# Another bank pair for the second block's output openings, and other points for the last attention heads, in a two-block fp32 kernel

## The chip, the cores and the metric

One core of a Trainium2 chip runs the whole program. The metric is the device time of one execution in microseconds, as the median of three runs. Matmuls run in fp32r on operands split in two parts; weights stream from HBM.

## The reference

Two blocks over 512 tokens of width 2048. The first is one layer with dilated attention (16 heads of 64) and a gated recurrence (8 heads), the second has two layers, each with retention (6 heads), differential attention (4 heads) and a gated linear recurrence (LRU).

```
# first block
z = rmsnorm(h) @ w_in;  y_att = o_att * silu(ag);  y_hg = rmsnorm(o_fw + o_bw) * silu(hg)
h = h + rmsnorm([y_att, y_hg] @ w_out);  h = h + rmsnorm(sigmoid(h @ w_pg) * (p @ w_pp))
# second block, for l in 0, 1
proj = rmsnorm(x) @ w_in[l]
w    = softmax(q0 k0) - lam * softmax(q1 k1);  do = w @ v               # causal, 4 heads
diff = rmsnorm(do) * g * (1 - lam_init) * silu(dg)
lru  = rg_lru(lx) * silu(lg)
x    = x + rmsnorm([ret, diff, lru] @ w_out[l])
```

## The kernel before

Activations stand transposed, as 16 row tiles of 128 x 512 (`MIX`, `UH`, `UL`). A projection is a chain of output tiles. For one tile TensorE makes 16 x 3 matmuls of 128 x 128 by 128 x 512: weight high by operand high, high by low, low by high. They fall into four **quarters** of 12 matmuls (`quarter`, L276 on). SyncE loads a tile's weights into one of two `w_raw` buffers; ScalarE rounds them into `w_high` quarter by quarter (`high`, L644), GpSimd subtracts into `w_low` (L230), and SyncE loads the next but one when GpSimd has finished. Every handover is a counting semaphore; each engine's order is written out in the program. `w_free` counts quarters that TensorE has used up, `z_free` accumulator tiles that were read out.

A **step** is four tiles, so 16 quarters (points p = 0 to 15), and behind each quarter the helper functions put a piece of the previous head's attention. Which piece stands at which point is in the tables `GROUPED`, `LAST_PAIR` and `LAST_DIF` (L80 to L89). A head of differential attention has four query blocks a: scores into SC (L497), a bias and row minimum on VectorE (L1370), two exponentials on ScalarE (L795), the weighted difference on VectorE (L1381), a turn on TensorE (L516), a copy out on ScalarE, and values into the bank `OB` (L507). Then the squares of `OB` on ScalarE (L780), their sum by a matmul with ones (L345), its inverse root on ScalarE (L663, L665) and the output on VectorE (L1358, L1360). With `GROUPED`, half a head's last blocks, its squares, sum, root and output fall into the next step (`late`). The last head has no next step, so `LAST_DIF` brings it to an end within its own: sum and output at p = 15. Its step runs beside four LRU gate tiles, for which VectorE scales the tile (`rstd_mul`, L1173), bounds it (L1185), waits for ScalarE's three activations (L675 to L679) and multiplies twice (L1192, L1441). Two more gate tiles follow without a head.

The output projection **opens** with two tiles together (`two_tiles`, `pair_step`, L313 to L334): for each row k of the operand six matmuls into Z[0] and Z[1], with the first tile's weights in `out_weights`. So an opening needs both banks free, and the operand row by row: ScalarE's copy `u_high` (L656) and VectorE's low part `u_low` (L1460). Rows 6 to 9 are the differential heads, rows 10 to 15 the LRU. The accumulators alternate by tile: the last gate tile stands in Z[1]. In the first block the opening's pair steps themselves stand between the pieces of the last attention pair (`LAST_PAIR`); there ScalarE and VectorE prepare operand rows around the step before and this one, with `low_quarter(q)` for rows 4q to 4q + 3, and values of a pair go to `OB`, free when VectorE has written the previous pair's output (L1278).

The PSUM has eight banks: Z[0], Z[1], SC[0], SC[1], TP[0], TP[1], `OB`, and `VB`, which holds a head's turned V until ScalarE copies it at point 4.

Of the kernel before, what the change touches and what calls it, by code (L numbers as in the profile page):

```python
# [27 lines left out]
ALU = mybir.AluOpType  # L28
AX = mybir.AxisListType

P = 128
# [40 lines left out]
             if any(max(LRU_BW * n, P * a) < min(LRU_BW * (n + 1), P * (a + 1)) and  # L72
# [45 lines left out]
def build(nc, wt, xT, pT, pos1, pos2, par1, par2, dlam, gw, cst, idn, masks, bias, dec, cmask, out):  # L118
    ctx = ExitStack()
    with ctx:  # L120
# [76 lines left out]
        OUT_BANK = SC[0]  # L197
        LAST = [SC[0], SC[1], TP[0], OB, Z[0], Z[1]]
# [78 lines left out]
        def _(pe):  # L277
# [35 lines left out]
            def pair_step(t, k, gen):  # L313
# [17 lines left out]
            def two_tiles(t, gen):  # L331

                for k in range(KT):
                    pair_step(t, k, gen)  # L334
# [86 lines left out]
            def att_values(j, a):  # L421

                if a == 0:
                    pe.wait_ge(sem("vn_ready"), j + 1)
                    pe.wait_ge(sem("att_done"), PRIMED + j)
                for hd in range(2):
                    pe.wait_ge(sem(f"pte{hd}"), PRIMED + j * 4 + a + 1)
                for c in range(4):
                    for hd in range(2):
                        mm = pe.matmul(OB[64 * hd:64 * hd + 64, a * P:(a + 1) * P],  # L430
# [13 lines left out]
            def att_work(j, p, late=None, at=GROUPED):  # L444
# [13 lines left out]
                if p in at["values"] and at is not GROUPED:  # L458
                    att_values(j, at["values"][p])
# [63 lines left out]
            def dif_work(j, p, late=None, at=GROUPED):  # L523

                if p == 0:
# [5 lines left out]
                if p in at["values"] and at is GROUPED:  # L531
# [5 lines left out]
                if p in at["values"] and at is not GROUPED:  # L537
                    dif_values(j, at["values"][p])
                if late is not None and p == at["sums"]:
                    dif_sums(late)  # L540
                if p == 15 and at is not GROUPED:
                    dif_sums(j)
# [60 lines left out]
            for l in range(LAYERS):  # L603
# [16 lines left out]
                with pe.Fori(2, DIF_HEADS) as i:  # L620
# [3 lines left out]
                     late=l * DIF_HEADS + DIF_HEADS - 2, at=LAST_DIF)  # L624
# [13 lines left out]
        def _(act):  # L638
# [147 lines left out]
            def dif_work(j, p, late=None, at=GROUPED):  # L786

                if p in at["softmax"]:
# [20 lines left out]
                if p == 15 and at is not GROUPED:  # L809
                    dif_squares(j)  # L810
                    dif_root(j)
# [1050 lines left out]
```

## Time and profile before

| | us |
|---|---|
| median of three runs | 3239.13 (3238.85 to 3240.21) |
| the profiled execution | 3240.39 |
| its span, first to last instruction | 3238.6 |
| TensorE busy | 3087.8 (95%) |
| VectorE, GpSimd, ScalarE busy | 1685.2, 1308.0, 1186.2 |
| mean granted TensorE clock | 0.983 of full |

A time in the rows below is in microseconds from the span's start. The first block's opening stands near 1060 to 1105, those of the second block's layers near 2157 and 3037.

### The profile page before, as it was taken

The numbers are of one execution on the slowest core, as the hardware profiler recorded it, in microseconds if no ns is written. First come the engines' busy times: TensorE is split into PE (matmuls) and PEld (weight loads), VectorE is DVE, ScalarE is ACT, GpSimd is POOL, SyncE is SP. The second block draws the span as 40 slices with busy tenths as digits, with TensorE's granted clock in tenths as the row PEclk, the third lists the DMA queues.
The fourth block names the chain that finished last, engine by engine and source line by source line (L and its number), as shares of the span: only waits on it lengthen the run. The fifth ranks groups of instructions, "written<-read, shape, count | busy, mean of one in ns | idle before, by whom it ended". The sixth has DMA issues, their size and how long they took to land.

```text
span 3238.6 us, 44470 instructions
## 1 busy us (share of the span) xinstructions
PE 3087.8 (95%) x15326; PEld 2434.9 (75%) x15326; DVE 1685.2 (52%) x2260; ACT 1186.2 (37%) x2092; POOL 1308.0 (40%) x1004
## 2 busy tenths in 40 slices
PE   8999999999999999998999999989999999999897
PEld 6877777777777787877777777768777777777785
DVE  5576767645445514656565664451265556644412
ACT  5433333233333433343233333343332333343432
POOL 4433333333334244452434344344534434443444
PEclk9999999999999999998999999999999999999998
DMA  6222221121222223233322222223332222221322
GB/s 233 104 92 77 68 74 65 65 79 69 74 78 78 106 102 136 87 115 114 127 71 96 70 90 79 77 79 142 117 136 95 91 75 89 82 78 69 126 105 91
DMA packets 60374, 307.68 MB, mean 95 GB/s; under 512 B 5601, under 2 KB 5985, under 8 KB 28897
## 3 DMA queue, kind: packets, MB, share of 16 engines
q1 hardware_dynamic: 34848, 253.77, 22.1%
q10 hardware_dynamic: 25408, 52.37, 4.6%
q8 instruction: 71, 1.16, 0.1%
q14 instruction: 47, 0.38, 0.0%
HBM read 287.77 MB, written 18.35 MB: 95 GB/s over the span
## 4 chain that ended last, share of the span: by engine, by line
issue 58%; POOL 30%; PE 9%; POOLq 1%; DMA 1%; ACT 1%; DVE 1%; DVEq 0%; SPq 0%; ACTq 0%
POOL w_low L230 29%; PE z L293 8%; PE z L326 1%; DMA w_raw<-in_wt 1%; POOLq L229 1%; ACT u_high L656 0%; PE scores L293 0%; POOL next_weights L238 0%; DVE u_low L1460 0%; POOLq L264 0%; DVE work L1179 0%; POOLq L252 0%; ACT w_high L644 0%; DVEq L1751 0%; DVE work L1753 0%
## 5 line engine op out<-in xcount | busy, mean ns | idle before, releaser
L230 POOL TENSOR_TENSOR w_low<-w_raw,w_high 128x512 fp32r<-128x512 f32 x932 | 1247.9, 1343 | 1904.9 <-ACT w_high L644 1893.9
L293 PE MATMUL z<-u_high,w_high 128*128 128x512 f32 x3408 | 1382.2, 406 | 4.7 <-POOL w_low L230 4.0
L293 PE MATMUL z<-u_high,w_low 128*128 128x512 f32 x3408 | 1333.3, 391 | 0.0
L293 PE MATMUL z<-u_low,w_high 128*128 128x512 f32 x3408 | 1332.6, 391 | 0.0
L644 ACT ACTIVATE w_high<-w_raw 128x512 fp32r<-128x512 f32 x928 | 577.5, 628 | 1342.2 <-PE z L293 1209.8
L293 PEld LDWEIGHTS z<-u_high,w_high 128*128 128x128 f32 x3408 | 643.2, 189 | 152.7 <-issue 15.2
L293 PEld LDWEIGHTS z<-u_low,w_high 128*128 128x128 f32 x3408 | 643.5, 189 | 143.4 <-issue 14.4
L293 PEld LDWEIGHTS z<-u_high,w_low 128*128 128x128 f32 x3408 | 642.4, 189 | 137.4
L1477 DVE TENSOR_TENSOR work<-work 128x512 f32<-128x512 f32 x87 | 92.3, 1061 | 364.9 <-ACT work L875 351.6
L1173 DVE TENSOR_TENSOR work<-z,work 128x512 f32<-128x512 f32 x110 | 76.1, 692 | 185.8 <-PE z L293 143.4
L1201 DVE SCALAR_TENSOR_TENSOR work<-z,work 128x512 f32<-128x512 f32 x56 | 38.7, 692 | 186.7 <-PE z L293 185.9
L1179 DVE RECIPROCAL work<-work 128x512 f32<-128x512 f32 x40 | 134.1, 3353 | 3.3 <-issue 0.4
L1205 DVE SCALAR_TENSOR_TENSOR work<-z,work 32x512 f32<-32x512 f32 (+1 forms) x176 | 120.9, 687 | 2.4
L1242 DVE TENSOR_TENSOR work<-work 128x512 f32<-128x512 f32 x64 | 70.6, 1102 | 81.6 <-PE scores L388 74.8
L309 PE MATMUL z<-u_high,next_weights 128*128 128x512 f32 x192 | 71.7, 415 | 20.4 <-DVE u_low L1462 12.8
L656 ACT ACTIVATE work<-work 128x512 f32<-128x512 f32 x56 | 37.8, 674 | 116.2 <-DVE work L1246 116.2
L656 ACT ACTIVATE work<-turned 128x512 f32<-128x512 f32 (+2 forms) x100 | 53.5, 543 | 72.9 <-PE turned L441 43.3
L388 PEld LDWEIGHTS scores<-work 128*32 128x32 f32 (+2 forms) x1792 | 38.5, 120 | 49.6 <-DVE work L1256 23.1
L388 PE MATMUL scores<-work 128*32 128x32 f32 (+2 forms) x1792 | 46.3, 210 | 25.7 <-DVE work L1256 11.9
L1192 DVE TENSOR_TENSOR mixed<-work 128x512 f32<-128x512 f32 (+1 forms) x35 | 24.3, 694 | 85.5 <-ACT work L679 85.5
L1209 DVE TENSOR_TENSOR work<-work 128x512 f32<-128x512 f32 x56 | 64.5, 1152 | 5.2
L675 ACT ACTIVATE work<-work 128x512 f32<-128x512 f32 x48 | 30.2, 629 | 93.1 <-DVE work L1185 93.1
(241 smaller groups left out, 3088.2 us busy)
## 6 DMA issues: line engine op xcount, KB each, us to landing
w_raw<-in_wt SPq DMA_DIRECT2D x242, 1024.0 KB, 4.8
out_hT<-work ACTq DMA_DIRECT2D x10, 1024.0 KB, 6.9
work<-in_xT ACTq DMA_DIRECT2D x8, 1024.0 KB, 13.2
work<-out_hT ACTq DMA_DIRECT2D x8, 1024.0 KB, 10.3
e_scratch<-work ACTq DMA_DIRECT2D x1, 4096.0 KB, 17.0
work<-in_gw ACTq DMA_DIRECT2D x2, 1792.0 KB, 10.5
work<-in_dec ACTq DMA_DIRECT2D x12, 256.0 KB, 2.6
work<-rope_tables ACTq DMA_DIRECT2D x10, 256.0 KB, 2.9
```

What stands on the lines that cost most here:

```text
L230: pool.tensor_tensor(WL[:, 4 * q:4 * q + 4, :], RAW[:, t.odd, 512 * q:512 * q + 512].rearrange("p (k c) -> p k c", k=4), WH[:, 4 * q:4 * q ...
L293: mm = pe.matmul(bank[:], w[:, k, :], u[:, k, :], start=(k == 0 and n == 0), stop=(k == KT - 1 and n == 2))
L309: mm = pe.matmul(bank[:], w[x], u[:, k, :], start=(k == 0 and n == 0), stop=(k == KT - 1 and n == 2))
L388: mm = pe.matmul(bank[o:o + g, keys], kk, qq, start=True, stop=True)
L644: act.activation(WH[:, 4 * q:4 * q + 4, :], RAW[:, n.odd, 512 * q:512 * q + 512].rearrange("p (k c) -> p k c", k=4), ACT.Copy).then_inc(se ...
L656: i = act.activation(dst, src, ACT.Copy, **kw)
L1173: v.tensor_tensor(dst, (Z[t.odd] if bank is None else bank)[:], row(RSTD), ALU.mult).then_inc(sem("z_free"), 1)
L1179: v.reciprocal(row(r), row(r))
L1205: i = v.scalar_tensor_tensor(out=row(TM)[o:o + half], in0=z[x:x + half, :], scalar=-scale if first else scale, in1=row(sin)[o:o + half], o ...
L1209: v.tensor_tensor(row(dst), row(dst), row(TM), ALU.add)
L1242: v.tensor_tensor(x, x, y, ALU.mult)
L1477: i = v.tensor_tensor(row(ACC), row(ACC), row(SQ0 + s), ALU.add)
```

## The change

Nothing is added to the computation. Four things move:

1. The second block's openings write `Z[0]` and `VB` instead of `Z[0]` and `Z[1]`, and wait for one accumulator tile fewer. ScalarE reads the second tile from `VB`.
2. In the second block the last differential head uses `GROUPED`. Its values of block 2 and turn of block 3 stand behind quarter 0 of gate tile 4, its values of block 3 behind quarter 0 of tile 5, its sum behind quarter 1 of tile 5. On ScalarE its copy, squares and root stand between the pieces of the output operand, on VectorE its output between low parts 7 and 8.
3. The last attention pair of the first block puts its values into `VB`.
4. In the first block VectorE scales the last gate tile before it makes any low part; low quarters 0 to 3 stand at points 0 to 3 of the last pair's step.

```diff
-LAST_DIF = dict(scores={0: 0, 3: 1, 7: 2, 11: 3}, softmax={1: 0, 4: 1, 8: 2, 12: 3}, turn={3: 0, 6: 1, 10: 2, 14: 3},
-                values={5: 0, 7: 1, 11: 2, 15: 3}, turn_late={0: 3}, values_late={0: 2, 2: 3}, last=2, sums=3, out=4, v_copy=2)
...
+        FIRST = {1: [Z[0], Z[1]], 2: [Z[0], VB]}
...
-                    pe.wait_ge(sem("z_free"), t.times(1, -T_HGG))
+                    pe.wait_ge(sem("z_free"), t.times(1, -T_HGG if block == 1 else -T_HGG - 1))
...
-                        mm = pe.matmul(Z[x][:], w[x], u[:, k, :], start=(k == 0 and n == 0),
+                        mm = pe.matmul(FIRST[block][x][:], w[x], u[:, k, :], start=(k == 0 and n == 0),
...
-                    pe.wait_ge(sem("att_done"), PRIMED + j)
+                    if bank is OB:
+                        pe.wait_ge(sem("att_done"), PRIMED + j)
...
-                    att_values(j, at["values"][p])
+                    att_values(j, at["values"][p], VB)
...
                 for m in range(4, LRU_TILES):
                     for q in range(4):
                         quarter(Tile(T_L2 + R_LG + m, (PER_LAYER, l)), q)
+                        if (m, q) == (4, 0):
+                            dif_values(last, 2)
+                            dif_turn(last, 3)
+                        if (m, q) == (5, 0):
+                            dif_values(last, 3)
+                        if (m, q) == (5, 1):
+                            dif_sums(last)
...
                 for q in range(4):
                     high(t.plus(-2), q)
+                    if q == 0:
+                        dif_turned(last, 3)
...
+                    if q == 2:
+                        act.wait_ge(sem("dif_done"), PRIMED + last + 1)
                     for m in range(4 * q, min(4 * q + 4, 15)):
                         copy(UH[:, m, :], MIX[:, m, :], "uh_ready")
+                    if q == 0:
+                        dif_squares(last)
+                    if q == 1:
+                        dif_root(last)
...
-                 between={14: lambda: low_quarter(0), 15: lambda: low_quarter(1)})
...
-                 between={0: lambda: low_quarter(2), 2: lambda: low_quarter(3), 6: lambda: low_tile(14, 16, MIX[:], None)})
+                 between={0: lambda: low_quarter(0), 1: lambda: low_quarter(1), 2: lambda: low_quarter(2),
+                          3: lambda: low_quarter(3), 6: lambda: low_tile(14, 16, MIX[:], None)})
...
                 low(l * 32 + 64, MIX[:], b=8)
+                dif_out(l * DIF_HEADS + DIF_HEADS - 1, 9)
+                low(l * 32 + 64, MIX[:], a=8, b=12)
                 rstd_mul(Tile(T_L2 + R_LG + 5, (PER_LAYER, l)), row(RW))
                 bounded()
-                low(l * 32 + 64, MIX[:], a=8, b=12)
```

TensorE, last layer, around the last head's sum of squares (`turned<-work,ones`). Before, behind quarter 15 of the head's step, with the last values ahead of it:

```order
L293 MATMUL z<-u_low,w_high 128x512
L293 MATMUL z<-u_high,w_low 128x512
L507 MATMUL o_bank<-work 128x128 [waits dpte]
L507 MATMUL o_bank<-work 128x128 x3
L345 MATMUL turned<-work,ones 128x512 [waits dsq_ready]
L293 MATMUL z<-u_high,w_high 128x512 [waits l_ready,z_free]
L293 MATMUL z<-u_low,w_high 128x512
L293 MATMUL z<-u_high,w_low 128x512
```

In the changed program, behind quarter 1 of the last gate tile:

```order
L290 MATMUL z<-u_high,w_low 128x512
L290 MATMUL z<-u_high,w_high 128x512
L290 MATMUL z<-u_low,w_high 128x512
L290 MATMUL z<-u_high,w_low 128x512
L342 MATMUL turned<-work,ones 128x512 [waits dsq_ready]
L290 MATMUL z<-u_high,w_high 128x512 [waits l_ready]
L290 MATMUL z<-u_low,w_high 128x512
L290 MATMUL z<-u_high,w_low 128x512
```

The sum has moved six quarters on; its wait for the squares (`dsq_ready`) now stands inside the last gate tile.

ScalarE, last layer, from the fifth gate tile's activations to the first copies of operand rows 8 to 11. Before:

```order
L675 ACTIVATE work<-work 128x512 [waits g_bounded]
L677 ACTIVATE work<-work,ones 128x512
L679 ACTIVATE work<-work 128x512
L644 ACTIVATE w_high<-w_raw 128x512 [waits w_free,w_raw1]
L656 ACTIVATE u_high<-mixed 128x512 x4
L644 ACTIVATE w_high<-w_raw 128x512 [waits w_free,w_raw1]
L656 ACTIVATE u_high<-mixed 128x512 x4
L644 ACTIVATE w_high<-w_raw 128x512 [waits w_free,w_raw1]
L656 ACTIVATE u_high<-mixed 128x512 [waits lru_done]
```

In the changed program (`work<-o_bank` are the squares, `work<-turned,constants` and the row behind it the root):

```order
L678 ACTIVATE work<-work 128x512 [waits g_bounded]
L680 ACTIVATE work<-work,ones 128x512
L682 ACTIVATE work<-work 128x512
L647 ACTIVATE w_high<-w_raw 128x512 [waits w_free,w_raw1]
L659 ACTIVATE u_high<-mixed 128x512 x4
L783 ACTIVATE work<-o_bank 128x512 [waits dav_done,dif_done]
L647 ACTIVATE w_high<-w_raw 128x512 [waits w_free,w_raw1]
L659 ACTIVATE u_high<-mixed 128x512 x4
L666 ACTIVATE work<-turned,constants 128x512 [waits dss_done]
L668 ACTIVATE work<-work 128x512
L647 ACTIVATE w_high<-w_raw 128x512 [waits w_free,w_raw1]
L659 ACTIVATE u_high<-mixed 128x512 [waits dif_done,lru_done]
```

The squares stand behind the first high part of the second output tile and its four operand copies, the root behind the next four; the copies of rows 8 to 11 also wait for the head's output.

VectorE, first block, from the last step before the last pair into it. Before:

```order
L1214 COPY work<-work 128x512
L1215 COPY work<-work 128x512
L1460 TENSOR_TENSOR u_low<-mixed,u_high 128x512 [waits uh_ready] x8
L1173 TENSOR_TENSOR work<-z,work 128x512 [waits w_free]
L1185 TENSOR_SCALAR work<-work 128x512
L1288 ISA work,small<-scores,work 128x512 [waits s_done,ones_set]
L1288 ISA small 128x1
L1288 ISA work,small<-scores,work 128x512 [waits s_done,ones_set]
L1288 ISA small 128x1
L1273 COPY work<-turned 128x512 [waits av_done,pt_done]
L1460 TENSOR_TENSOR u_low<-mixed,u_high 128x512 [waits uh_ready] x4
```

In the changed program:

```order
L1225 COPY work<-work 128x512
L1226 COPY work<-work 128x512
L1184 TENSOR_TENSOR work<-z,work 128x512 [waits w_free]
L1196 TENSOR_SCALAR work<-work 128x512
L1299 ISA work,small<-scores,work 128x512 [waits s_done,ones_set]
L1299 ISA small 128x1
L1299 ISA work,small<-scores,work 128x512 [waits s_done,ones_set]
L1299 ISA small 128x1
L1284 COPY work<-turned 128x512 [waits av_done,pt_done]
L1470 TENSOR_TENSOR u_low<-mixed,u_high 128x512 [waits uh_ready] x4
L1304 RECIPROCAL small<-small 128x2 [waits exp_done]
L1307 TENSOR_SCALAR work<-work,small 128x512 x2
```

The scaling of the last gate tile (L1173, now L1184) stands first, and the eight low parts behind the turned copy (L1273, now L1284) and the first probabilities.

## Rows read from the trace of the kernel before

**Rows 1.** The page: section 1, and of section 6 the weight loads (KB each, us to landing).

```profile
PE 3087.8 (95%) x15326; PEld 2434.9 (75%) x15326; DVE 1685.2 (52%) x2260; ACT 1186.2 (37%) x2092; POOL 1308.0 (40%) x1004
...
w_raw<-in_wt SPq DMA_DIRECT2D x242, 1024.0 KB, 4.8
```

**Rows 2.** Waits of TensorE over the span: us in total, times, longest.

```profile
PE z L326 <- DVE work L1173: 18.1, 3, 7.4
...
PE o_bank L507 <- issue: 11.7, 2, 5.9
...
PE turned L516 <- DVE work L1381: 5.7, 4, 1.8
...
PE turned L345 <- ACT work L780: 1.5, 2, 0.7
```

**Rows 3.** TensorE's time line from 2961: start, duration, instruction, [idle before <- releaser].

```profile
2967.49 0.77 PE L507 MATMUL o_bank<-work 128*128 128x128 f32 x2 [5.85 <-issue]
2967.91 0.77 PE L293 MATMUL z<-u_high,w_high 128*128 128x512 f32 x1
...
2973.15 0.39 PE L516 MATMUL turned<-identity,work 128*128 128x128 f32 x2
```

**Rows 4.** TensorE's time line, later places of the same step and the opening.

```profile
2950.64 1.05 PE L507 MATMUL o_bank<-work 128*128 128x128 f32 x8
2951.45 0.48 PE L293 MATMUL z<-u_high,w_high 128*128 128x512 f32 x1
...
2987.74 0.55 PE L516 MATMUL turned<-identity,work 128*128 128x128 f32 x3 [1.75 <-DVE work L1381]
...
3037.44 0.80 PE L326 MATMUL z<-u_high,out_weights 128*128 128x512 f32 x1 [7.40 <-DVE work L1173]
...
3041.42 0.39 PE L326 MATMUL z<-u_high,w_high 128*128 128x512 f32 x1
3041.64 0.39 PE L326 MATMUL z<-u_low,w_high 128*128 128x512 f32 x1
```

**Rows 5.** VectorE's time line, the first gate scaling of the last head's step.

```profile
2954.47 0.69 DVE L1173 TENSOR_TENSOR work<-z,work 128x512 f32<-128x512 f32 x1 [3.64 <-PE z L293]
```

**Rows 6.** Time lines of TensorE (first row) and ScalarE beside the last gate tile.

```profile
3019.00 0.39 PE L293 MATMUL z<-u_high,w_high 128*128 128x512 f32 x1
...
3006.47 0.60 ACT L780 ACTIVATE work<-o_bank 128x512 f32<-128x512 f32 x1 [0.26 <-PE o_bank L507]
...
3026.13 0.63 ACT L644 ACTIVATE w_high<-w_raw 128x512 fp32r<-128x512 f32 x1 [2.14 <-DMA w_raw<-in_wt]
...
3028.76 0.62 ACT L644 ACTIVATE w_high<-w_raw 128x512 fp32r<-128x512 f32 x1
```

**Rows 7.** TensorE's time line behind a pause of 4.10 us.

```profile
1513.80 0.80 PE L293 MATMUL turned<-u_high,w_high 128*128 128x512 f32 x1 [4.10 <-POOL w_low L230]
...
1519.06 0.39 PE L293 MATMUL turned<-u_high,w_high 128*128 128x512 f32 x1
```

**Rows 8.** VectorE's time line at the opening of the last output projection.

```profile
3027.46 9.15 DVE L1460 TENSOR_TENSOR u_low<-mixed,u_high  x8
3036.69 0.69 DVE L1173 TENSOR_TENSOR work<-z,work 128x512 f32<-128x512 f32 x1
...
3041.78 2.49 DVE L1460 TENSOR_TENSOR u_low<-mixed,u_high  x4
```

**Rows 9.** First block's opening: time lines of VectorE (two rows), then of TensorE.

```profile
1059.76 6.17 DVE L1460 TENSOR_TENSOR u_low<-mixed,u_high 128x512 fp32r<-128x512 f32 x8
...
1078.11 0.68 DVE L1273 COPY work<-turned 128x512 f32<-128x512 f32 x1
...
1066.76 0.50 PE L326 MATMUL z<-u_high,out_weights 128*128 128x512 f32 x1 [3.28 <-DVE work L1173]
...
1071.47 1.64 PE L430 MATMUL o_bank<-work 128*64 128x128 f32 x16 [1.56 <-ACT work L656]
...
1078.93 1.09 PE L430 MATMUL o_bank<-work 128*64 128x128 f32 x16 [0.96 <-DVE work L1273]
```

More of the change, by code:

```diff
@@ L311, in three_tiles, with pair_step @@
                     mm.then_inc(sem("w_free"), 3)
-            def pair_step(t, k, gen):
+            def pair_step(t, k, gen, block=1):
                 q = k // 4
                 if k == 0:
-                    pe.wait_ge(sem("z_free"), t.times(1, -T_HGG))
+                    pe.wait_ge(sem("z_free"), t.times(1, -T_HGG if block == 1 else -T_HGG - 1))
                 if k % 4 == 0:
@@ L333, in two_tiles @@
                 for k in range(KT):
[L334 removed]
+                    pair_step(t, k, gen, 2)
             def third_tiles(t):
@@ L419, in att_scores, with att_values @@
                               start=True, stop=True).then_inc(sem("s_done"), 1)
-            def att_values(j, a):
+            def att_values(j, a, bank=OB):
                 if a == 0:
                     pe.wait_ge(sem("vn_ready"), j + 1)
-                    pe.wait_ge(sem("att_done"), PRIMED + j)
+                    if bank is OB:
+                        pe.wait_ge(sem("att_done"), PRIMED + j)
                 for hd in range(2):
@@ L429, in att_values @@
                     for hd in range(2):
-                        mm = pe.matmul(OB[64 * hd:64 * hd + 64, a * P:(a + 1) * P],
+                        mm = pe.matmul(bank[64 * hd:64 * hd + 64, a * P:(a + 1) * P],
                                        row(VN)[:, c * P + 64 * hd:c * P + 64 * hd + 64],
@@ L521, in dif_sums, with dif_work @@
                 sum_rows(row(NRO), TP[1], (sem("dsq_ready"), j + 1), "dss_done")
-            def dif_work(j, p, late=None, at=GROUPED):
+            def dif_work(j, p, late=None):
+                at = GROUPED
                 if p == 0:
@@ L530, in dif_work @@
                     dif_values(late, at["values_late"][p])
-                if p in at["values"] and at is GROUPED:
+                if p in at["values"]:
                     dif_values(j, at["values"][p])
@@ L623, in _ @@
                 step(Tile(T_L2 + R_LG, (PER_LAYER, l)), work="dif", j=l * DIF_HEADS + DIF_HEADS - 1,
-                     late=l * DIF_HEADS + DIF_HEADS - 2, at=LAST_DIF)
+                     late=l * DIF_HEADS + DIF_HEADS - 2)
+                last = l * DIF_HEADS + DIF_HEADS - 1
                 for m in range(4, LRU_TILES):
@@ L784, in dif_root, with dif_work @@
                 inv_root(TP[1], row(NRO), P, (sem("dss_done"), j + 1), "dro_ready")
-            def dif_work(j, p, late=None, at=GROUPED):
+            def dif_work(j, p, late=None):
+                at = GROUPED
                 if p in at["softmax"]:
@@ L878, in out_slots @@
                 for s in range(2):
-                    one(t.plus(s), s, s, n, s == 0 or pair, taken=t.times(4, 8) if pair else None)
+                    one(t.plus(s), s, s, n, s == 0 or pair, taken=t.times(4, 8) if pair else None, bank=FIRST[1 if n == 16 else 2][s])
                     if loads:
@@ L1116, in _ @@
                 step(Tile(T_L2 + R_LG, (PER_LAYER, l)), gates=l * 16 + 26, work="dif", j=l * DIF_HEADS + DIF_HEADS - 1,
-                     late=l * DIF_HEADS + DIF_HEADS - 2, at=LAST_DIF)
+                     late=l * DIF_HEADS + DIF_HEADS - 2)
+                last = l * DIF_HEADS + DIF_HEADS - 1
                 t = Tile(T_L2 + R_OUT + l * PER_LAYER)
@@ L1273, in att_turned, with att_out @@
                 v.tensor_copy(row(PT + 1), TP[1][:]).then_inc(sem("pte1"), 1)
-            def att_out(j):
+            def att_out(j, bank=OB):
                 v.wait_ge(sem("av_done"), PRIMED + j * 4 + 4)
-                v.tensor_tensor(MIX[:, j + 8, :], OB[:], MIX[:, j + 8, :], ALU.mult).then_inc(sem("att_done"), 1)
+                v.tensor_tensor(MIX[:, j + 8, :], bank[:], MIX[:, j + 8, :], ALU.mult).then_inc(sem("att_done"), 1)
             def att_work(j, p, late=None, at=GROUPED):
@@ L1304, in att_work @@
                 if p == 15 and at is not GROUPED:
-                    att_out(j)
+                    att_out(j, VB)
             def lru_work(j, p, b):
@@ L1361, in dif_out, with dif_work @@
                                        op0=ALU.mult, op1=ALU.mult).then_inc(sem("dif_done"), 1)
-            def dif_work(j, p, m=None, late=None, at=GROUPED):
+            def dif_work(j, p, m=None, late=None):
+                at = GROUPED
                 if p in at["scores"]:
@@ L1384, in dif_work @@
                     dif_out(late, m - 1)
-                if p == 15 and at is not GROUPED:
-                    dif_out(j, m)
             WORK = {"hg": hg_work, "att": att_work, "ret": ret_work, "dif": dif_work}
```

11 lines of the change are left out of this document (2 added, 9 removed).

## The prediction

> **What bounds the kernel now.** I read the page first: TensorE is busy for 95% of the span [rows 1], so what can be won back is its idle places, and the stretches that it runs at the lower clock. The view of waits then says which of them the edit touches [rows 2]: 18.1 us in three waits at L326, the output openings, for a VectorE scaling (L1173); 11.7 us in two waits at L507, and 5.7 and 1.5 us in small waits of the last differential head (L516, L345). The reader should see that the largest waits of the list stand in the last steps before the output projections, and nowhere else does the diff touch TensorE.
>
> The time line of TensorE shows what a wait costs beyond itself. At 2967.49 it resumes after 5.85 us, and from 2967.91 to 2973.15 twelve matmuls take 5.24 us [rows 3], 0.43 each, where later ones start 0.23 apart (3041.42, 3041.64 [rows 4]). That is 1.2 GHz instead of 2.4 and costs 2.4 us against 12 x 0.23 + 0.1. Behind the last layer's opening wait of 7.40 us nine matmuls take 3.98, from 3037.44 to 3041.42 [rows 4], for about 2.15: 1.8 us. The first layer's two long waits are as long as these, since the view of waits has 11.7 = 2 x 5.85, and 18.1 less the first block's 3.28 [rows 9] is 2 x 7.4. I put their clock at the same 2.4 and 1.8.
>
> So the second block holds 11.7 + 5.7 + 1.5 + 14.8 = 33.7 us of waits and 2 x (2.4 + 1.8) = 8.4 us of clock: **42 us** over two layers within reach of these edits.
>
> **The last differential head.** It takes the grouped points; its last values, last turn and sum of squares move behind quarters of the two last gate tiles. Nothing is added or removed. Its first values (L507) waited for the previous head's output, until 13.0 us after VectorE's gate scaling at 2954.47 (2967.49) [rows 3, 5]. They stood behind quarter 5 and now stand behind quarter 8: three quarters later, each 12 x 0.227 = 2.7 us, and the wait was 5.85. That leaves 8.2 - 5.85 = 2.3 us of slack; VectorE has nothing more to do before that output, which stays behind the second probabilities. So **-11.7 and its clock -4.8**. The turns waited 1.75 us at most [rows 4], three quarters or fewer behind the gate quarter that held VectorE; now they come two quarters, 5.4 us, later: **-5.7**. The 1.5 us before the old sum go with it. If this cover fails, the next late thing is ScalarE, which now has the previous head's root behind the second pair of exponentials.
>
> **The sum at its new point is the new wait.** Call M the start of the last gate tile on TensorE, 3019.00 [rows 6]. TensorE then does quarter 0, the last values (2950.64 to 2951.45, 0.8 us [rows 4]), quarter 1, and wants the squares at M + 2 x 2.72 + 0.9 = M + 6.3. ScalarE makes them only behind the first quarter of the output operand: in its order come the high part that waits for its load until 3026.13, then four u_high copies, and the next instruction starts at 3028.76 [rows 6]. There the squares now stand, 0.60 us [rows 6], so they are ready at 3029.4 = M + 10.4. The load takes 4.8 us [rows 1] and starts when the last gate tile's weights are used up, so all of this moves with M. TensorE waits **4.1 us from start to start, 3.9 shown as idle**, in each layer.
>
> Does the clock fall there? The nearest pause in length is one of 4.10 us: twelve matmuls from 1513.80 to 1519.06 take 5.26 [rows 7], 2.4 us lost, the same as after 5.85. Below it lie the 1.75 us pause with nothing lost, which gives the bound 0, and I take 2.4. By the Trainium skill, page "TensorE: Matmul & The Clock Gate", section "What's actually happening", the number of cold matmuls at the start of one kernel came out as 6, 11 or 14 in different runs. By those counts this term would be an estimated 1.2 to 2.8 us per layer, and the sum up to 2.4 us lower or 0.8 higher; the trace's twelve lie inside.
>
> **The opening.** It wrote Z[0] and Z[1] and waited until the last gate tile was scaled out of Z[1], at 3036.69, behind low parts 0 to 7 (9.15 us) [rows 8]. With v_bank it needs only the tile before that, scaled long ago. Behind the sum TensorE has quarters 2 and 3, so it opens at M + 10.4 + 0.5 + 5.4 + 2.4 = M + 18.7; today 3037.44 = M + 18.4. It opens no earlier, but what it waited for is now work. The operand is there: rows 0 to 7 by M + 17.6 [rows 8]. Then come the head's output and four copies on ScalarE (about 4 us; a high part and four copies fit between 3026.13 and 3028.76, rows 6), low parts 8 to 11 (2.5), and what today stands between 3036.69 and 3041.78 + 2.49, 7.6 us [rows 8]: at most M + 31.7. TensorE uses a row in 1.36 us and wants row 12 at M + 35. So **-14.8 and -3.6**, with 3 us to spare.
>
> Second block: 42.1 - 2 x (3.9 + 2.4) = **29.5 us won**.
>
> **The first block.** The last gate tile is scaled at about 1059.8, since the eight low parts that took 6.17 us from there [rows 9] go behind it. The opening then waits for row 0, behind the scores and the turned copy, until about 1065 instead of 1066.76, and the 1.56 us at 1071.47 go, since ScalarE's sigmoid comes 5 us earlier. But VectorE works without a pause from 1059.76 to the copy at 1078.11 [rows 9], and the first values of the last pair wait for that copy (1078.93). Of all that work only two low parts go behind it, 2 x 0.62 = 1.2 us: copy done at about 1077.6. TensorE, ready near 1072.4 (three pair steps, scores, values, turn), waits 5 us in one piece, instead of 3.28, 1.56 and 0.96. By rows 3 and 7 that costs 2.4 us of clock where now nothing is lost. Net **+1.2 us**; bounds -1.2 (the clock stays up) and +3.
>
> Here a rule bears on the low parts. Alone four take 2.49 us, 0.62 each, beside GpSimd's low parts eight take 9.15, 1.14 each [rows 8]. By the Trainium skill, "SBUF — State Buffer", section "Who interferes with whom", a VectorE instruction with two SBUF inputs and a GpSimd instruction that reads SBUF block each other fully. By it I would price four more of them at 1.14, an estimated 2 us, and the first block at 3 instead of 1.2. It adds to the upper bound only.
>
> **Sum.** 3240.4 (the profiled execution) - 29.5 + 1.2 = 3212.1. The median of the runs shown is 1.3 below the profiled one, so **3211 us**, 28 us or 0.9% faster.
>
> **Rivals.** (a) *No wait at the sum, or the clock holds.* With the squares in time 12.6 us more are won, less up to 6 because the opening at M + 12.3 then wants row 12 before M + 31.7: 3198 to 3204. With the clock alone held, 3206. No row speaks for the first; for the second only the unslowed short pauses. 12%.
> (b) *The moved places pass their waits on.* Turns or values of the last head stall again because ScalarE has exponentials, root and sigmoid in a row, or rows 8 to 15 come late at the opening. Half of 18.9 us (11.7 + 5.7 + 1.5) kept gives 3220, with 3 us more per layer at the opening 3226. Slack of 2 to 3 us at three places speaks against it. 11%.
> (c) *The opening isn't freed.* It still pauses 7.4 us, for weights or operand rows instead of the bank, and this besides the new wait: 3211 + 14.8 + 3.6 = 3229. Low part 0 starts at 3027.46 [rows 8], before the tile's end, against it. 4%.
> (d) *Slower than before*, by the sum's wait alone. It hangs on the load of the second output tile, for which TensorE now stands still. Each layer has 14 us to lose: it ties when the load takes 19 us instead of 4.8 [rows 1], and is 6.5 us slower at 22. Its landing at 3026.13 [rows 6] shows nothing of the kind. 2%.
>
> **How the numbers follow.** My forecast, the wait at the sum with a fallen clock, has 71% and spans 3205 to 3217: clock 0 to 2.8 twice, the wait 3 to 5 twice, first block -1.2 to +3. The range goes on into (a) and (b) until about 18% is left out: 3202 to 3222. 0.2% is 6.5 us, about what a measurement of this kernel can tell from no change. All cases but (d) are faster by more than that; for waits that I haven't seen I take 3% off: faster 0.95, same 0.03, slower 0.02.
>
> **What would show it.** Right: L507's waits gone and no idle above 1 us in the last head's step; one wait of about 4 us per layer at the sum matmul (now L342), for the squares of L783, then some twelve matmuls 0.43 apart; the opening (L323) without a wait in both layers; in the first block one pause of about 5 us before the last pair's first values. Wrong: no pause at L342 or one above 6 us; a wait at L323 for u_low or w_low in the second block; a new wait at L505 or L514.

## The result and the profile after

| | before | after |
|---|---|---|
| median of 4 runs each, us | 3238.99 (3236.34 to 3240.21) | **3207.53** (3206.78 to 3208.13) |
| the profiled execution, us | 3240.39 | 3206.78 |
| its span | 3238.6 | 3205.0 |
| mean granted TensorE clock | 0.983 | 0.987 |

The ratio is 0.9904, with a 95% interval from 0.9887 to 0.9921: 31.5 us or 1% faster, 3.5 us below the forecast of 3211.

First the page of the changed kernel, the line of section 1.

```profile
PE 3078.9 (96%) x15326; PEld 2428.9 (76%) x15326; DVE 1681.9 (52%) x2260; ACT 1184.6 (37%) x2092; POOL 1304.2 (41%) x1004
```

Against [rows 1] the same 15326 matmuls keep TensorE busy 8.9 us less: that is for the most part clock. The rest of the 33.6 us of span is idle time. The view of waits shows which, again for TensorE (us in total, times, longest):

```profile
PE turned L342 <- ACT work L783: 8.0, 2, 4.0
...
PE v_bank L428 <- DVE work L1284: 5.3, 1, 5.3
```

Of [rows 2] the waits of the last head for values and turns (now L505 and L514) are gone, and so are the 18.1 us at the opening for VectorE's scaling (now L323 for L1184). What L323 still has are two waits for low parts, 2.1 us together and both in the first block's opening; the openings of the second block have none. The sum has a new wait, 4.0 us in each layer, for the squares of L783.

How a whole tail went is best read with one view, busy time by stretch, from the first turn of the last head's step to the third tile of the projection. Each line has the stretch and its length, then busy time and count of PE, PEld, DVE, ACT and POOL, TensorE's clock, the DMA share and GB/s. The kernel before, first block's opening step to its next stage, then the two tails:

```profile
1059.72:1269.53 209.81, 195.82 (x929) 156.54 (x929) 60.42 (x101) 77.68 (x142) 92.02 (x70) 0.98 0.30 105
2062.42:2180.72 118.30, 101.28 (x446) 80.05 (x444) 55.58 (x85) 51.03 (x96) 42.55 (x31) 0.94 0.20 72
2943.03:3061.14 118.11, 101.44 (x446) 80.19 (x444) 54.27 (x77) 51.03 (x96) 42.42 (x31) 0.94 0.20 72
```

The same three stretches of the changed kernel:

```profile
1058.60:1269.12 210.52, 195.60 (x929) 156.59 (x929) 59.63 (x101) 77.50 (x142) 91.22 (x70) 0.97 0.29 105
2061.24:2164.05 102.81, 98.79 (x445) 78.94 (x444) 54.80 (x85) 50.63 (x96) 41.96 (x31) 0.97 0.24 82
2925.04:3027.74 102.70, 98.72 (x445) 78.90 (x444) 52.91 (x77) 50.51 (x96) 41.72 (x31) 0.97 0.23 82
```

Length less PE's busy time is idle time. In the last tail it goes from 118.11 - 101.44 = 16.67 to 102.70 - 98.72 = 3.98, and the busy time falls by 2.72 because less of it is at the lower clock. So the two tails give 15.5 + 15.4 = **30.9 us**; the first block's stretch is 0.7 longer. That makes 30.2 us. The other 3.4 us of the span lie in stretches that the edit doesn't touch: TensorE stands 1.12 us earlier already at 1058.60, ahead of the first edit. There TensorE is busy 3.5 us less with the same matmuls, so they are stretches at the lower clock that come out longer in one profiled execution than in another. The medians differ by 31.5 us.

At the end of the last tail TensorE's time line reads:

```profile
2986.39 0.39 PE L290 MATMUL z<-u_high,w_high 128*128 128x512 f32 x1
...
2989.11 1.05 PE L505 MATMUL o_bank<-work 128*128 128x128 f32 x8
...
2996.88 2.08 PE L342 MATMUL turned<-work,ones 128*128 128x512 f32 x2 [3.98 <-ACT work L783]
...
2999.18 0.63 PE L290 MATMUL z<-u_low,w_high 128*128 128x512 f32 x1
...
3002.55 0.40 PE L290 MATMUL z<-u_high,w_high 128*128 128x512 f32 x1
...
3005.99 0.39 PE L323 MATMUL z<-u_high,out_weights 128*128 128x512 f32 x1
```

The last gate tile starts at 2986.39; the prediction calls this time M. The last values at 2989.11 carry no bracket, so they didn't wait, and neither does the opening at 3005.99. Between them stands the one pause, and behind it the lower clock, 1.2 GHz instead of 2.4: from 2999.18 to 3002.55 eight matmuls take 3.37 us, 0.42 each. Beside it, ScalarE and then VectorE:

```profile
2993.64 0.63 ACT L647 ACTIVATE w_high<-w_raw 128x512 fp32r<-128x512 f32 x1 [2.26 <-DMA w_raw<-in_wt]
2994.17 2.17 ACT L659 ACTIVATE u_high<-mixed 128x512 fp32r<-128x512 f32 x4
2996.25 0.57 ACT L783 ACTIVATE work<-o_bank 128x512 f32<-128x512 f32 x1
```

```profile
2994.96 6.82 DVE L1470 TENSOR_TENSOR u_low<-mixed,u_high  x8
...
3009.05 0.69 DVE L1184 TENSOR_TENSOR work<-z,work 128x512 f32<-128x512 f32 x1
```

The squares' operand, the last values, was complete by 2990.2, but ScalarE stood in its order before the high part that waited for its load. The load is only part of the delay: ScalarE is idle for it for 2.26 us, then rounds and makes four copies, and starts the squares 2.61 us after 2993.64. By these rows the squares would have ended near 2994.6 with the load there at once, an estimate, still 1.7 us after TensorE came for them (2996.88 - 3.98 = 2992.90). And VectorE scales the last gate tile at 3009.05, 3.1 us **after** the opening: with the old bank TensorE would stand there (experiment 2).

### The profile page after: what moved, and what is told of

Read it like the earlier page. It is cut to its first block, busy times and chain, and to the rows that moved or that the text cites. A ratio compares the mean times of both kernels' runs of the same rounds, so it can differ in the third digit from the quotient of the medians.

```text
span 3205.0 us, 44471 instructions
## 1 busy us (share of the span) xinstructions
PE 3078.9 (96%) x15326; PEld 2428.9 (76%) x15326; DVE 1681.9 (52%) x2260; ACT 1184.6 (37%) x2092; POOL 1304.2 (41%) x1004
## 4 chain that ended last, share of the span: by engine, by line
issue 58%; POOL 30%; PE 9%; POOLq 1%; DMA 1%; ACT 1%; DVE 0%; DVEq 0%; SPq 0%; ACTq 0%
POOL w_low L227 29%; PE z L290 8%; DMA w_raw<-in_wt 1%; POOLq L226 1%; PE scores L290 0%; PE v_bank L323 0%; PE z L323 0%; POOL next_weights L235 0%; ACT u_high L659 0%; PE turned L342 0%; POOLq L261 0%; DVE work L1190 0%; POOLq L249 0%; DVEq L1762 0%; DVE work L1764 0%
## 5 line engine op out<-in xcount | busy, mean ns | idle before, releaser
L1184 DVE TENSOR_TENSOR work<-z,work 128x512 f32<-128x512 f32 x110 | 76.1, 692 | 165.2 <-PE z L290 124.9
L306 PE MATMUL z<-u_high,next_weights 128*128 128x512 f32 x192 | 71.0, 411 | 21.2 <-DVE u_low L1472 13.2
L385 PE MATMUL scores<-work 128*32 128x32 f32 (+2 forms) x1792 | 46.4, 210 | 25.6 <-DVE work L1267 11.8
L678 ACT ACTIVATE work<-work 128x512 f32<-128x512 f32 x48 | 30.2, 630 | 94.6 <-DVE work L1196 94.6
```

The lines of the kernel that those rows point to most:

```text
L306: mm = pe.matmul(bank[:], w[x], u[:, k, :], start=(k == 0 and n == 0), stop=(k == KT - 1 and n == 2))
L385: mm = pe.matmul(bank[o:o + g, keys], kk, qq, start=True, stop=True)
L1184: v.tensor_tensor(dst, (Z[t.odd] if bank is None else bank)[:], row(RSTD), ALU.mult).then_inc(sem("z_free"), 1)
```

## The experiments

The first four kernels take the second block apart; ratios are to the kernel before, measured on the same chip in the same round. Where a time is set against the change's 3207.53, the two come from different rounds; the kernel before had a median of 3238.99 beside the change, 3238.78 in the rounds of experiments 1 to 4 and 3240.14 in those of 5 to 8, so such a difference is known to 1 or 2 us.

**1. The bank alone** (`bank_only`): the kernel before, with the second block's openings in Z[0] and VB and the wait for one tile fewer (ScalarE's read of the second tile follows, not shown).

```diff
+        FIRST = {1: [Z[0], Z[1]], 2: [Z[0], VB]}
...
-                    pe.wait_ge(sem("z_free"), t.times(1, -T_HGG))
+                    pe.wait_ge(sem("z_free"), t.times(1, -T_HGG if block == 1 else -T_HGG - 1))
...
-                        mm = pe.matmul(Z[x][:], w[x], u[:, k, :], start=(k == 0 and n == 0),
+                        mm = pe.matmul(FIRST[block][x][:], w[x], u[:, k, :], start=(k == 0 and n == 0),
```

> The kernel before with the other bank for the second block's openings and nothing else. Theory: the two opening waits of 7.4 us and their clock go whole, since the operand rows keep ahead of the opening (row 12 is ready near 3042.4, wanted at 3046), 18.5 us in all: about 3220; the waits at L507, L516 and L345 stay. Rival 1: the operand takes the bank's place as limit, the opening stops for u_low, and less than 12 us are won (above 3227). Rival 2: the bank alone brings nothing (3239).

Measured: 3221.43 us (3219.51 to 3222.07), ratio 0.9946 (0.9929 to 0.9962), 17.4 us faster. Its waits of TensorE:

```profile
PE o_bank L508 <- issue: 11.7, 2, 5.9
...
PE turned L517 <- DVE work L1382: 5.7, 4, 1.8
...
PE z L327 <- DVE work L1174: 3.3, 1, 3.3
```

The two opening waits are gone, only the first block's 3.3 is left of [rows 2]'s 18.1, and the head's own waits stand as they were. VectorE's order is unchanged, which shows how far the bank was from being free:

```profile
3025.34 0.69 DVE L1174 TENSOR_TENSOR work<-z,work 128x512 f32<-128x512 f32 x1
```

TensorE opened at 3018.45, 6.9 us ahead of that scaling. So the bank alone turns 7.4 us of waiting per layer and the clock behind it into work, and the operand rows are there: no wait for a low part stands in the second block's openings.

**2. The change with the old bank** (`old_bank`): everything moved, but the openings in Z[0] and Z[1] again, with their old wait.

```diff
-        FIRST = {1: [Z[0], Z[1]], 2: [Z[0], VB]}
+        FIRST = {1: [Z[0], Z[1]], 2: [Z[0], Z[1]]}
...
-                    pe.wait_ge(sem("z_free"), t.times(1, -T_HGG if block == 1 else -T_HGG - 1))
+                    pe.wait_ge(sem("z_free"), t.times(1, -T_HGG))
```

> The changed kernel with Z[0] and Z[1] for the second block's openings again. Theory: with the head's sum inside the last gate tile, that tile's end and its scaling on VectorE (done at 3009.74 in the changed kernel's trace, the opening began at 3005.99) lie only 3.7 us apart, so the old bank costs 3.7 us of wait and about 2 us of clock per layer: 3219. Rival 1: the bank is worth its full 9.2 us per layer here too: 3226. Rival 2: nothing (3207.5), since the sum's wait has taken its place.

Measured: 3219.89 us (3215.46 to 3221.06), ratio 0.9938 (0.9921 to 0.9954). Its waits:

```profile
PE turned L342 <- ACT work L783: 8.1, 2, 4.2
...
PE z L323 <- DVE work L1184: 7.2, 2, 3.6
```

The waits at values and turns go without the bank's help, and the opening still waits for the scaling, but 3.6 us instead of 7.4:

```profile
3016.71 0.79 PE L323 MATMUL z<-u_high,out_weights 128*128 128x512 f32 x1 [3.62 <-DVE work L1184]
```

Counted from the start of the last gate tile (3019.00 in before [rows 6], 2993.26 here), TensorE wants to open at 19.8 instead of 11.0 us, since the values, the sum with its 4 us of waiting and the clock behind that now lie within this tile. The scaling frees the bank at 23.4 instead of 18.4, since the head's output and low parts 8 to 11 now stand ahead of it. TensorE comes 8.8 us later, the bank 5.0, and the wait is 3.8 shorter. So the two halves don't add up. The tails tell it best, since they leave out the clock of the rest of the run. Those of this kernel:

```profile
2062.59:2169.72 107.13, 99.32 (x445) 79.36 (x444) 52.43 (x85) 50.72 (x96) 41.82 (x31) 0.97 0.22 79
2931.91:3040.05 108.14, 100.60 (x446) 79.97 (x445) 51.82 (x77) 50.61 (x96) 41.38 (x31) 0.95 0.22 78
```

They are 118.30 + 118.11 - 107.13 - 108.14 = 21.1 us shorter than before's; those of `bank_only`, 108.90 and 108.41, are 19.1 shorter, and the change's 30.9. That is 9.3 less than the sum of the two: 7.6 of it is the part of the opening's idle time that the moved places have already removed, twice 3.8; the rest may be the clock behind it, which wasn't taken apart. By the medians 17.4 and 18.9 stand against 31.5, only 4.8 less; each median is off its tails by 0.6 to 2.2 us, which lie outside them. On top of the moved places the bank is worth 12.4 us by the medians and 9.8 by the tails.

**3. A later point for the sum** (`sum_late`): the sum two quarters later, behind the last gate quarter. If TensorE only asks for the squares too early, the wait goes, and the opening must then be ready some 7 us sooner.

```diff
-                        if (m, q) == (5, 1):
+                        if (m, q) == (5, 3):
                             dif_sums(last)
```

> The changed kernel with the last head's sum matmul behind quarter 3 of the last gate tile instead of quarter 1. Theory: TensorE comes to the sum at M + 11.8, the squares are ready at M + 10.4, so the 4.0 us wait and its 3.1 us of clock go in both layers: 14 us less, 3193, and no new wait at the opening (row 8 is ready near M + 18, wanted at M + 23; row 12 near M + 26, wanted at M + 29). Rival 1: the operand rows become the limit, since head output and low parts follow a later root: a wait for u_low of 1 to 4 us per layer, 3195 to 3202. Rival 2: the clock falls somewhere else anyway: 3199.

Measured: 3195.28 us (3193.99 to 3195.8), ratio 0.9865 (0.9848 to 0.9881), 12.3 us below the change. Both tails:

```profile
2061.68:2157.48 95.80, 95.80 (x446) 77.33 (x444) 54.92 (x85) 50.41 (x96) 43.04 (x31) 1.00 0.25 88
2919.16:3014.96 95.80, 95.80 (x445) 77.34 (x444) 51.72 (x77) 50.31 (x96) 42.68 (x31) 1.00 0.25 88
```

Length and busy time are equal and the clock is 1.00: TensorE doesn't stand for one moment from the head's first turn to the third tile, so rival 1, operand rows that come late, is out, though its range reached down to the measured time. 95.80 us is the floor of this stretch with these instructions, and gives the price of everything else: before, 118.11 = 95.80 + 16.67 idle + 5.64 busy at the lower clock; after, 102.70 = 95.80 + 3.98 + 2.92. (The last term is busy time beyond the floor; a little of it is the edge of each pause and not clock, see below.)

**4. Earlier squares** (`squares_early`): TensorE's order as in the change, but ScalarE makes the squares ahead of the operand's first quarter and of the high part that waits for its load.

```diff
                 gate_sigmoid(l * 16 + 30)
+                dif_squares(last)
...
-                    if q == 0:
-                        dif_squares(last)
```

> The changed kernel with the last head's squares on ScalarE straight behind the fifth gate tile's activations, ahead of the high part that waits for its load. Theory: the sum's wait is made by the squares' place behind that load; ready at M + 5.5 against M + 6.3 the wait goes, 14 us less: 3193, as with a late sum. Rival 1: the wait is made by the values' own chain (copy of the turned block, values in quarter 0) and stays: 3207. Rival 2: the root, now earlier, delays u_high copies and the opening stops for operand rows: 3196 to 3200.

Measured: 3194.34 us (3194.14 to 3194.97), ratio 0.9861 (0.9845 to 0.9878). ScalarE's time line has the squares ahead of the load:

```profile
2986.39 0.58 ACT L783 ACTIVATE work<-o_bank 128x512 f32<-128x512 f32 x1
2988.74 0.63 ACT L647 ACTIVATE w_high<-w_raw 128x512 fp32r<-128x512 f32 x1 [1.77 <-DMA w_raw<-in_wt]
```

Here too both tails take 95.80 us. Two cures at the two ends of one wait give the same, so the wait is what was said: the place of the squares in ScalarE's order, behind a high part that waits for its load and four operand copies. It isn't the gate tile, the values or the operand. The two causes of the late squares, load and copies, weren't moved apart.

The other four take the first block apart.

**5. The second block only** (`second_only`): the change, with the first block as before (low quarters at their old points, shown here; last pair in OB, the edit of experiment 6).

```diff
-                 late=PAIRS - 3)
+                 late=PAIRS - 3,
+                 between={14: lambda: low_quarter(0), 15: lambda: low_quarter(1)})
...
-                 between={0: lambda: low_quarter(0), 1: lambda: low_quarter(1), 2: lambda: low_quarter(2),
-                          3: lambda: low_quarter(3), 6: lambda: low_tile(14, 16, MIX[:], None)})
+                 between={0: lambda: low_quarter(2), 2: lambda: low_quarter(3), 6: lambda: low_tile(14, 16, MIX[:], None)})
```

> The changed kernel with the first block as it was (old order of the low parts, last pair in the old bank). Theory: the first block's edit moves three pauses into one and wins or costs under 1 us, so the time stays at 3207 (3205.5 to 3208.5), and its first block shows the pauses of 3.3, about 1.6 and 1 to 2.5 us again. Rival 1: the first block's edit is worth its 3.6 us of earlier pauses: 3211. Rival 2: it costs 3 us: 3204.5.

Measured: 3207.55 us (3206.16 to 3208.62), ratio 0.9901 (0.9886 to 0.9916), which can't be told from the change's 0.9904. Its trace has the stretch of the first block at 209.88 us against 210.52 with the change, 0.6 us:

```profile
1058.69:1268.57 209.88, 195.39 (x928) 155.62 (x929) 60.38 (x101) 77.70 (x142) 92.05 (x70) 0.98 0.30 105
```

The three traces with the old first block have 209.78 to 209.88 us for this stretch, the five with the new one and its pause of 5.3 us 210.20 to 211.38. So the first block's edits give nothing and may cost up to 1.6 us; all of the gain is the second block's. The pauses came back as 3.3, 0.4 and 2.5 us, so of the three expected the middle one, about 1.6, was off.

**6. The last pair back in OB** (`pair_bank_back`): the change without its edit 3.

```diff
-                    att_values(j, at["values"][p], VB)
+                    att_values(j, at["values"][p])
...
-                    att_out(j, VB)
+                    att_out(j)
```

> The changed kernel with the last attention pair's values in the old bank (so they also wait for the previous pair's output). Theory: that output ends 0.7 us before the turned copy that the values wait for anyway, on the same engine, so nothing changes: one pause of 5.3 us, released by the copy (L1284 there), 3207. Rival: the bank is what the first block's edit lives from, and the pause grows by 1 us or more.

Measured: 3209.11 us (3208.65 to 3209.58, two runs), ratio 0.9905 (0.9887 to 0.9923), no difference. The pause is to the hundredth the one of the change:

```profile
PE o_bank L428 <- DVE work L1284: 5.3, 1, 5.3
```

The previous pair's output is written at 1075.24, right ahead of the copy at 1075.85 in VectorE's order. Whoever waits for the copy has waited for the bank.

**7. Low quarters further apart** (`lows_later`): the change, with the low quarters at points 0, 3, 6 and 8 and row 14's at 9, so that only one of them stands ahead of the copy.

```diff
-                 between={0: lambda: low_quarter(0), 1: lambda: low_quarter(1), 2: lambda: low_quarter(2),
-                          3: lambda: low_quarter(3), 6: lambda: low_tile(14, 16, MIX[:], None)})
+                 between={0: lambda: low_quarter(0), 3: lambda: low_quarter(1), 6: lambda: low_quarter(2),
+                          8: lambda: low_quarter(3), 9: lambda: low_tile(14, 16, MIX[:], None)})
```

> The changed kernel with the first block's low quarters 1, 2 and 3 at points 3, 6 and 8 of the last pair's step and tile 14 at 9, so that VectorE copies the first turned block ahead of eight more low parts. Theory: the 5.3 us pause is VectorE's queue; the copy ends near 1071.5 of the changed kernel's trace instead of 1076.5, the pause goes and the clock with it: 7 to 8 us less, 3200. Rival 1: the pause only moves to the second values or to row 4 or 8 of the operand: 2 to 4 us less, 3204 to 3206. Rival 2: ScalarE's exponentials, not VectorE's low parts, set the copy: no change, 3207.

Measured: 3199.89 us (3198.85 to 3200.28), ratio 0.9875 (0.986 to 0.989), as the theory had it. VectorE's time line of the change, around the copy (L1284):

```profile
1063.01 3.58 DVE L1470 TENSOR_TENSOR u_low<-mixed,u_high 128x512 fp32r<-128x512 f32 x4
...
1067.72 2.49 DVE L1470 TENSOR_TENSOR u_low<-mixed,u_high 128x512 fp32r<-128x512 f32 x4
...
1072.65 2.49 DVE L1470 TENSOR_TENSOR u_low<-mixed,u_high 128x512 fp32r<-128x512 f32 x4
1075.24 0.69 DVE L1289 TENSOR_TENSOR mixed<-o_bank,mixed 128x512 f32<-128x512 f32 x1
1075.85 0.68 DVE L1284 COPY work<-turned 128x512 f32<-128x512 f32 x1
```

and TensorE's there, behind it that of this kernel:

```profile
1076.68 1.98 PE L428 MATMUL v_bank<-work 128*64 128x128 f32 x16 [5.29 <-DVE work L1284]
```

```profile
1071.61 1.09 PE L428 MATMUL v_bank<-work 128*64 128x128 f32 x16
...
1098.77 0.50 PE L323 MATMUL z<-u_high,out_weights 128*128 128x512 f32 x1 [0.58 <-DVE u_low L1470]
```

Eight low parts, 4.98 us, stood between TensorE and the copy. Behind it they are still in time; the 0.58 us at 1098.77 stand in before (1106.13) and in the change (1105.73) too. The stretch falls from 210.52 to 203.36:

```profile
1058.73:1262.09 203.36, 193.68 (x928) 155.10 (x929) 59.35 (x101) 77.48 (x142) 91.64 (x70) 0.99 0.30 109
```

**8. Both** (`both`): experiments 4 and 7 together.

> The changed kernel with the squares early (as squares_early) and the low quarters later (as lows_later). Theory: the two repairs stand 1000 us apart and add up: 3194.3 - 7.5 = 3187, no wait of TensorE over 1 us in either place. Rival 1: the first block's repair gives only its idle time or less (3190 to 3192). Rival 2: they don't add, a later stage waits for the same loads and gives it back: 3194.

Measured: **3187.14 us** (3186.65 to 3189.75, five runs), ratio 0.9839 (0.9825 to 0.9852), 53 us below before's 3240.14 in the same rounds and 20 below the change. The two gains against the change were 13.2 and 7.6 us and would give 3186.7: within the 1 to 2 us they are independent. The three stretches, the tails again at their floor:

```profile
1059.05:1262.67 203.62, 193.75 (x928) 155.13 (x929) 59.69 (x101) 77.59 (x142) 91.74 (x70) 0.99 0.30 109
2054.88:2150.68 95.80, 95.80 (x446) 77.35 (x444) 55.92 (x85) 50.44 (x96) 43.21 (x31) 1.00 0.25 88
2911.81:3007.61 95.80, 95.80 (x446) 77.35 (x444) 52.65 (x77) 50.34 (x96) 42.76 (x31) 1.00 0.25 88
```

## Why the prediction was right, step by step

**The last head's cover held.** The prediction took 11.7 and 5.7 us off because the values had 2.3 us of slack and the turns three quarters or fewer. The sum's 3.98 us are all the idle time that the last tail has (102.70 - 98.72), so the head's step has none, and `old_bank` shows that this is the moved places' doing. Rival (b), waits passed on, is excluded by that and by the openings without a wait. The prediction's remark that the largest waits of the list stand in the last steps was too wide: 13.9 us at L566, 12.8 at L309 and 11.9 at L388 are as large and lie elsewhere (13.6, 13.2 and 11.8 after). No term hung on it.

**The sum's wait was right in size and cause.** It put the squares at M + 10.4 and TensorE's wish at M + 6.3. The last gate tile starts at M = 2986.39; TensorE stood from 2992.90, M + 6.5, and the squares ended at 2996.82, M + 10.4. The shown idle is 3.98 against 3.9, from start to start 4.14 against 4.1. Experiments 3 and 4 confirm the mechanism from either end.

**Clock and pause edges were sized too small; this is the term that missed.** The prediction asked "Does the clock fall there?" and took twelve slow matmuls, 2.4 us. From the sum to the opening TensorE took 3005.99 - 2996.88 = 9.11 us. In `squares_early` the same instructions take 6.35 at full speed:

```profile
2987.85 1.02 PE L342 MATMUL turned<-work,ones 128*128 128x512 f32 x2
2988.31 0.80 PE L290 MATMUL z<-u_high,w_high 128*128 128x512 f32 x1
2988.95 0.40 PE L290 MATMUL z<-u_low,w_high 128*128 128x512 f32 x1
...
2994.20 0.39 PE L323 MATMUL z<-u_high,out_weights 128*128 128x512 f32 x1
```

So 2.76 us were lost to the clock in the last layer, where the term had 2.4. That the two are near is in part luck, for the make-up is another: eight projection matmuls were slow and not twelve, 1.56 us, and the other 1.20 were lost by the sum's two and the one behind them, which take 2.30 us to 2999.18 and 1.10 here. Besides, the first matmul behind a sum holds TensorE for 0.64 us and not 0.23 even at full speed, which the prediction's 0.5 + 5.4 left out. Both together are the 0.8 us by which 9.11 exceeds its 8.3.

Before was priced too low as well. The floor gives 5.64 us of busy time too much, where the prediction had 4.2 of clock. An estimate of the difference: the matmul ahead of a pause is shown busy for 0.39 us where in a row one starts each 0.23, so a pause costs 0.16 more than the idle time shown, 0.8 for the five in that tail; the other 0.6 is clock behind values and turns, since [rows 3, 4] were counted on projection matmuls alone. After has one pause and 0.16 of this. Per layer the busy time fell by 2.72 in the last layer and 2.49 in the first, where the sum had 1.8: 1.6 us in both, less 0.2 because the idle time fell a little less than the 25.9 it had. These 1.4 us are what the second block gave beyond its 29.5. Both sides of the difference were priced too low, 5.64 for 4.2 before and 2.92 for 2.4 after, so part of the error cancelled. The Trainium skill, "TensorE: Matmul & The Clock Gate", section "What's actually happening", has 6, 11 or 14 cold matmuls at one kernel's start; the numbers here spread in a like way inside a kernel, from seven to fourteen, as the last section shows.

**The opening.** It was expected at M + 18.7 without a wait and came at M + 19.6, without one: 0.1 from the squares, 0.8 from the term above. Its rows were there throughout. Rival (c) is excluded by this, and in its strongest form by `bank_only`, where the opening passes VectorE's scaling by 6.9 us.

**The low parts.** The prediction carried over 9.15 us for eight of them [rows 8]. They took 6.82, which left the operand more slack than it assumed and changed no term.

**The first block.** It expected the last pair's values 1.2 us earlier, one pause of 5 us, and behind it 2.4 us of clock "where now nothing is lost", +1.2 in all. The values start 18.08 us into the stretch instead of 19.21, the pause is 5.29 us, and the stretch is 0.7 longer. The size came out near, but this step was wrong, and its agreement is luck. The stretch up to the values, before and then after:

```profile
1059.72:1078.93 19.21, 13.42 (x78) 9.10 (x79) 18.10 (x32) 10.13 (x22) 3.46 (x2) 0.91 0.15 56
1058.60:1076.68 18.08, 11.32 (x79) 7.67 (x79) 16.15 (x30) 10.14 (x22) 2.82 (x2) 0.92 0.18 59
```

TensorE is busy 2.1 us longer in before, mostly at the lower clock (the four score matmuls at 1068.34 take 1.57 us, those of the change at 1065.40 only 1.13), so the pauses cost clock already: in the whole stretch the busy time hardly changes, 195.82 to 195.60, against 193.68 in `lows_later`. What grows is the idle time, by 0.9 us. Beside the 5.29 us the change waits at row 0 of the opening,

```profile
1063.84 0.47 PE L323 MATMUL z<-u_high,out_weights 128*128 128x512 f32 x1 [1.47 <-DVE u_low L1470]
```

which the prediction had in its path ("until about 1065") but not among its pauses: 1.47 + 5.29 = 6.76 us against 3.28 + 1.56 + 0.96 = 5.80 [rows 9].

The Trainium skill's rule that a VectorE instruction with two SBUF inputs and a GpSimd read block each other ("SBUF — State Buffer", "Who interferes with whom") had been priced at four more low parts of 1.14, so +3. The direction can be seen: the first four low parts took 3.58 us against 2.49 while GpSimd had one subtraction beside them:

```profile
1063.30 1.54 POOL L227 TENSOR_TENSOR w_low<-w_raw,w_high 128x512 fp32r<-128x512 f32 x1 [3.33 <-ACT w_high L647]
```

But that was the only one, and the other eight ran at 0.62; a rule on overlap must be priced by how much overlap there is, not by the dearest row (three stretches of low parts lost 0.7 to 0.8 us for each us of GpSimd's subtraction beside them).

**Rival (a)**, no wait at the sum, didn't occur by itself, but experiments 3 and 4 made it. Its 3198 to 3204 kept back up to 6 us for late operand rows. None were late: 3194 to 3195. **Rival (d)** needed a late load. The high part ahead of the squares did wait for its load, until 2993.64, M + 7.3, and this with the work behind it makes only the 4 us; how the wait grows with a slower load wasn't tried.

**The sum.** Predicted -29.5 and +1.2 on the profiled execution; the tails gave -30.9, the first block +0.7, and -3.4 lie where nothing was changed. That last part no edit can be credited with. Without it the profile would stand at 3240.4 - 30.2 = 3210.2, against 3212.1. The prediction's bounds, all taken at once, give about 3202 to 3216, and not the 3205 to 3217 that it states for its own case; 3207.5 lies in both.

## What to carry to other kernels

Where a product opens in a bank that a slow reader still holds, look for a bank whose last reader is done: choosing another one cost nothing here, and alone it gave 17 us. When a step is moved, look at what stands ahead of its operand's producer in that engine's order; a small operation behind one that waits for a load inherits the load's wait and the work that follows it, and one line moved ahead of them was worth 13 us. Find the floor of a stretch (busy time equal to its length at clock 1.00) and price idle time and clock against it, which catches the edges of pauses that a count of slow matmuls misses.

## What the runs showed of the hardware

The time lost to the clock behind one and the same pause differs from execution to execution by more than 1 us. The place of [rows 7], which no kernel here changes, has a pause of 4.1 us in each. In before twelve matmuls took 5.26 us behind it, 2.5 more than at full speed. In `second_only` only seven were slow, from 1514.11 to 1517.16, 1.5 more. In the changed kernel the first three ran at full speed and the next nine, from 1514.19 on, at or near half:

```profile
1513.39 0.50 PE L290 MATMUL turned<-u_high,w_high 128*128 128x512 f32 x1 [4.08 <-POOL w_low L227]
...
1514.19 0.55 PE L290 MATMUL turned<-u_high,w_high 128*128 128x512 f32 x1
...
1517.84 0.39 PE L290 MATMUL turned<-u_high,w_high 128*128 128x512 f32 x1
```

Twelve took 1517.84 - 1513.39 = 4.45 us, 1.7 more than at full speed. In `pair_bank_back` fourteen were slow, from 1514.59 to 1520.70, 2.9 us more:

```profile
1514.59 0.79 PE L290 MATMUL turned<-u_high,w_high 128*128 128x512 f32 x1 [4.09 <-POOL w_low L227]
...
1520.70 0.40 PE L290 MATMUL turned<-u_high,w_low 128*128 128x512 f32 x1
```

In the same execution the first layer's pause at the sum, 4.00 us like the others, was followed by the upper clock soon (matmuls 0.23 apart from 2138.60 on), and its tail took 101.42 us instead of 102.8. By this, two profiled executions of equal kernels can differ by some 3 us, an estimate that fits the 3.4 us found above; the kernel before alone gave 3237.95 to 3241.26 us in seven executions of one round. A gain of that size should not be read from a single pair of profiles.

The other thing is the low parts: eight take 9.15 us in before [rows 8] and 6.82 after, at 0.62 each alone. In before they run beside four of GpSimd's subtractions, in after beside two. Where the same instructions stand in time to GpSimd's was worth 2.3 us of VectorE's time, and nothing on TensorE's path.
